# The borders of a feed-forward stage: VectorE's and ScalarE's orders by when TensorE needs each result, drains put off into the next pair, and two weight loads ahead of stores

## The reference, cut to what matters

```python
def swiglu_ffn(h, w_gate_up, w_down):
    gu = h @ w_gate_up                      # 1024 x 1024 by 1024 x 5632
    return (jax.nn.silu(gu[..., :D_FF]) * gu[..., D_FF:]) @ w_down   # D_FF = 2816
...
x = x + swiglu_ffn(rms_norm_2(x, norm_ffn[i]), ffn_w_gate_up[i], ffn_w_down[i])
return rms_norm_2(x, final_norm)
```

## Time and profile before

| what | value |
|---|---|
| median of three runs | 2220.53 us |
| the profiled execution | 2221.11 us, span 2219.3 us |
| TensorE matmul busy | 2047.9 us, 92% of the span |
| VectorE, ScalarE, GpSimd busy | 1422.1, 1007.3, 646.0 us |
| the stage `tail` (part with pairs) | 1540 to 2135 us of the span |
| TensorE's granted clock over the span | 0.958 of full |

### The profile page before, as it was taken

The page is one execution under the profiler, slowest core; times in us unless marked ns, Lnnn a source line. Parts: engine busy times, 40 slices in busy tenths (PEclk is TensorE's granted clock), DMA queues, the critical chain, the costliest instruction groups (busy, mean ns, idle before and its releaser), DMA issues. The chain is left out here.

```text
span 2219.3 us, 44505 instructions
## 1 busy us (share of the span) xinstructions
PE 2047.9 (92%) x15592; PEld 1533.1 (69%) x15592; DVE 1422.1 (64%) x1892; ACT 1007.3 (45%) x1513; POOL 646.0 (29%) x469
## 2 busy tenths in 40 slices
PE   5999989897598999988979989999899999999998
PEld 4788867686354555544558866678788888878787
DVE  6888627524578888877746448646755555474654
ACT  5212248302377788877722027723433333343334
POOL 1333311220000000000025632214444444454543
PEclk9999989998699999999979999999999999999999
DMA  7643114225999699999952310021233233264233
GB/s 275 239 164 126 39 52 167 107 77 219 401 420 422 254 391 423 422 422 422 380 190 95 95 34 1 1 95 57 81 100 105 98 113 99 85 229 145 100 122 125
DMA packets 100476, 410.06 MB, mean 185 GB/s; under 512 B 10444, under 2 KB 21548, under 8 KB 75436
## 3 DMA queue, kind: packets, MB, share of 16 engines
q1 hardware_dynamic: 81100, 366.53, 43.4%
q10 hardware_dynamic: 13968, 23.07, 2.8%
q0 software_dynamic: 5328, 19.40, 2.2%
HBM read 357.53 MB, written 51.43 MB: 184 GB/s over the span
## 5 line engine op out<-in xcount | busy, mean ns | idle before, releaser
L1712 PE MATMUL moe_hu<-x_res,acc_sq 128*32 128x256 f32 x5120 | 320.0, 392 | 25.0 <-DVE acc_sq L1631 12.4
L1609 DVE COPY x_res<-moew_raw 128x2048 f32 x243 | 269.7, 1136 | 105.8 <-PE moe_hu L1712 53.0
L1712 PEld LDWEIGHTS moe_hu<-x_res,acc_sq 128*32 128x32 f32 x5120 | 159.9, 112 | 144.4 <-issue 37.0
L1609 ACT ACTIVATE x_res<-moew_raw 128x2048 f32 (+1 forms) x121 | 197.9, 1636 | 34.2 <-DMA moew_raw<-in_w 24.0
L2584 PE MATMUL ff_bank<-xh,ff_u_hi 128*128 128x512 f32 x480 | 188.6, 393 | 9.9 <-DVE x_res L3065 6.6
L2546 POOL TENSOR_TENSOR ff_u_lo<-ff_sums,ff_u_hi 128x512 fp32r<-128x512 f32 x120 | 165.4, 1390 | 94.6 <-ACT ff_u_hi L2712 94.6
L2584 PE MATMUL ff_bank<-xh,ff_u_lo 128*128 128x512 f32 x480 | 187.5, 391 | 0.0
L2584 PE MATMUL ff_bank<-xl,ff_u_hi 128*128 128x512 f32 x480 | 187.5, 391 | 0.0
L2546 POOL TENSOR_TENSOR ff_u_lo<-ff_raw,ff_u_hi 128x512 fp32r<-128x512 f32 x90 | 122.9, 1366 | 215.2 <-ACT ff_u_hi L2712 215.2
L1620 ACT ACTIVATE moe_wdown<-moew_raw 128x2048 f32 x80 | 153.4, 1918 | 52.1 <-PE moe_y L1723 43.6
L1723 PE MATMUL moe_y<-moe_wdown,moe_at 128*32 128x256 f32 x2560 | 155.4, 384 | 2.2 <-ACT moe_at L1757 2.2
(11 more groups left out here) (489 smaller groups left out, 4615.7 us busy)
## 6 DMA issues: line engine op xcount, KB each, us to landing
moew_raw<-in_w SPq DMA_DIRECT2D x192, 1024.0 KB
ff_raw<-in_w_up SPq DMA_DIRECT2D x44, 512.0 KB, 3.6
blk_scratch<-x_res SPq DMA_DIRECT2D x56, 256.0 KB, 4.0
mid_w_raw<-in_w_qkv SPq DMA_DIRECT2D x24, 512.0 KB
in_w_raw<-in_w_in SPq DMA_DIRECT2D x23, 512.0 KB, 3.6
xbc<-in_w_ada SPq DMA_DIRECT2D x20, 512.0 KB, 8.5
y_scratch<-moe_ysb ACTq DMA_DIRECT2D x80, 128.0 KB, 6.8
ff_raw<-in_w_down SPq DMA_DIRECT2D x16, 512.0 KB, 3.6
```

Of the source, the lines that this page charges most:

```text
L1609: m = e.activation(to, src, ACT.Copy) if k == "act" else e.tensor_copy(to, src)
L1712: m = e.matmul(hu[u % 2][rows(j), 0:2 * FW].rearrange("p (a f) -> p a f", a=2), xt[:, t, rows(u)], w[:, :, FW * j:FW * (j + 1)], start=(t ...
```

## The change

The amount of computation stays the same on every engine. Orders and waits change.

- **SyncE, start of the stage.** `load_gate(2)` and `load_up(2)` are issued before the first store of pair 0; before, `load_up(2)` came behind it.
- **SyncE, first border.** `load_up(23)` comes before both stores of `LAST`.
- **ScalarE.** At the borders the blocks' high parts move to other places among the weights' high parts, and silu of `LAST`'s second half moves behind blocks 5 and 6.
- **VectorE, first border.** Blocks 0 to 3 are done before the first drain of pair 22. The rest of `LAST`'s gate moves into pair 22: the first half's `times_up` and the second half's sum behind drain p2, the second half's `times_up` behind drain p5.
- **VectorE, second border.** Blocks 0 to 3 are done in pair 25, and the drains p3, p5 and p6 of pair 25 move into pair 26.
- **Drains** now count on one semaphore, in the order of the list `drains`; `is_drained(e, c, p)` waits for the place of a drain in it. The four x tiles' wait is put on drains p2 and p6 as well.

```diff
+            drains = [(NPR, p) for p in range(7)]
+            for c in range(NPR + 1, NPR + NDN):
+                if c in borders:
+                    drains += [(c, p) for p in (0, 1, 2, 4)]
+                elif c - 1 in borders:
+                    drains += [(c, 0), (c, 1), (c, 2), (c - 1, 3), (c - 1, 5), (c, 3), (c, 4), (c, 5), (c - 1, 6), (c, 6)]
+                else:
+                    drains += [(c, p) for p in range(7)]
+            is_drained = lambda e, c, p: e.wait_ge(s_drained, drains.index((c, p)) + 1)
...
                     load_up(Q(1))
-                    after_even(Q(1))
+                    load_gate(Q(2))
+                    load_up(Q(2))
+                    store(Q(0), 0, 0, 0)
+                    store_mix(Q(0), 1)
...
                     load_block(0, 6)
+                    load_up(Q(NPR + 1))
                     store(LAST, 1, 0)
-                    load_up(Q(NPR + 1))
                     store(LAST, 1, 1)
...
+                    block_high(0, 0)
                     high(nq, 0)
                     high(nq, 1)
-                    block_high(0, 0)
+                    block_high(0, 1)
                     high(nq, 2)
                     high(nq, 3)
-                    block_high(0, 1)
+                    block_high(0, 2)
                     gate(q, 1, 0)
+                    block_high(0, 3)
                     high(nq, 4)
-                    block_high(0, 2)
                     high(nq, 5)
-                    gate(q, 1, 1)
-                    block_high(0, 3)
                     block_high(0, 4)
...
+                    def last_pair(n):
+                        if n == 0:
+                            sum_weights(pair_at(LAST, 1))
+                            block_low(0, 0)
+                            gate_sum(LAST, 1, 0)
+                            corner(LAST, 1)
+                            by_root(LAST, 1, 0, lambda: step.wait(e, LAST, 1), scaled)
+                            block_low(0, 1)
+                            block_low(0, 2)
+                            block_low(0, 3)
+                        elif n == 1:
+                            by_root(LAST, 1, 0, lambda: silu.wait(e, LAST, 1), step)
+                            times_up(LAST, 1, 0, 2)
+                        elif n == 2:
+                            gate_sum(LAST, 1, 1)
+                            by_root(LAST, 1, 1, lambda: step.wait(e, LAST, 3), scaled)
+                        else:
+                            by_root(LAST, 1, 1, lambda: silu.wait(e, LAST, 2), step)
+                            times_up(LAST, 1, 1, 4)
...
+                    def opening(c, left):
+                        n = borders[c - 1]
+                        drain(c, 0)
+                        block_low(n, 4)
+                        drain(c, 1)
+                        block_low(n, 5)
+                        drain(c, 2)
+                        left(0)
+                        drain(c, 3)
+                        block_low(n, 6)
+                        drain(c, 4)
+                        sum_weights(Q(c + 1))
+                        drain(c, 5)
+                        left(1)
+                        drain(c, 6)
+
+                    def inner(c):
+                        drain(c, 0)
+                        drain(c, 1)
+                        sum_weights(Q(c + 1), (0,))
+                        drain(c, 2)
+                        sum_weights(Q(c + 1), (1, 2, 3))
+                        for p in range(3, 7):
+                            drain(c, p)
+
+                    def ending(c):
+                        n = borders[c]
+                        drain(c, 0)
+                        drain(c, 1)
+                        sum_weights(Q(c + 1), (0,))
+                        drain(c, 2)
+                        sum_weights(Q(c + 1), (1, 2, 3))
+                        block_low(n, 0)
+                        drain(c, 4)
+                        for b in range(1, 4):
+                            block_low(n, b)
...
+                    def left_of_down(n):
+                        for p in ((3, 5), (6,))[n]:
+                            drain(NPR + FF_DOWN - 1, p)
```

More of the change, by code:

```diff
@@ L2391, in tail @@
             kept, scaled, silu, act_done = (PerPair(st, n, k) for n, k in (("kept", 3), ("scaled", 2), ("silu", 2), ("a", 2)))
-            c22, step, mixed, drained = (PerPair(st, n, k) for n, k in (("c22", 1), ("step", 4), ("mixed", 2), ("drained", 7)))
+            c22, step, mixed = (PerPair(st, n, k) for n, k in (("c22", 1), ("step", 4), ("mixed", 2)))
+            s_drained = st.sem("drained")
             halves = [(h, j) for h in range(2) for j in range(KT)]
@@ L2650, in _ @@
                             else:
-                                drained.wait(e, *{0: (before, 7), 1: (before, 6), 2: (d, 1), 3: (before, 4), 4: (d, 3), 5: (d, 2), 6: (d, 5)}[p])
+                                is_drained(e, *{0: (c - 2, 6), 1: (c - 2, 5), 2: (c, 0), 3: (c - 2, 3), 4: (c, 2), 5: (c, 1), 6: (c, 4)}[p])
                             if c - 1 in borders:
@@ L2836, in _ @@
                         high(q, 6)
+                        if c - 1 in borders:
+                            block_high(borders[c - 1], 5)
+                            block_high(borders[c - 1], 6)
                         if c == NPR:
-                            block_high(0, 5)
-                            block_high(0, 6)
-                        if c == NPR + FF_DOWN:
-                            block_high(1, 6)
+                            gate(LAST, 1, 1)
                         for p in range(6 if q != LASTD else 0):
                             high(pair_at(q, 1), p)
-                            if c == NPR + FF_DOWN - 1 and p < 5:
-                                block_high(1, p)
-                        if c == NPR + FF_DOWN - 1:
-                            block_high(1, 5)
+                            if c in borders and p in (0, 1, 3, 4, 5):
+                                block_high(borders[c], (0, 1, 2, 2, 3, 4)[p])
                     for k in range(FF_LAST):
@@ L2884, in _ @@
                     st.dve.start(e)
-                    for n in (summed, scaled, act_done, c22, step, mixed, drained):
+                    for n in (summed, scaled, act_done, c22, step, mixed):
                         n.start(e)
@@ L3052, in _, with drain @@
                         pair(Q(c), c % 2, mix=False)
-                    pair(LAST, 1, mix=False, between=lambda n: block_low(0, n))
-                    block_low(0, 2)
-                    def drain(q, p):
-                        d, (ja, jb) = down_pair(q), down_tiles(q)
+                    def last_pair(n):
[17 more added lines that the diff above has]
+                            times_up(LAST, 1, 1, 4)
+                    last_pair(0)
+                    def drain(c, p):
+                        q, (ja, jb) = Q(c), down_tiles(Q(c))
                         j, h = ((ja, 0), (jb, 1), (ja, 1), (ja, 0), (jb, 1), (ja, 1), (jb, 0))[p]
                         prod.wait(e, q, p + 1)
-                        if q[1] < NPR + FF_DOWN and j < K2 and p in (0, 1):
+                        if c < NPR + FF_DOWN and j < K2 and p in (0, 1, 2, 6):
                             e.wait_ge(s_kept[j], 32)
                         if p in (3, 4, 5):
-                            drained.wait(e, d, {3: 1, 4: 2, 5: 3}[p])
+                            is_drained(e, c, {3: 0, 4: 1, 5: 2}[p])
                         to = x[:, j, span(h)]
-                        drained.done(e.tensor_tensor(to, XYZ[q[1] % 2][(0, 1, 0, 2, 0, 1, 0)[p]], to, ALU.add))
+                        e.tensor_tensor(to, XYZ[c % 2][(0, 1, 0, 2, 0, 1, 0)[p]], to, ALU.add).then_inc(s_drained, 1)
                     def plane_low(k):
@@ new lines, in closing, with left_of_up @@
+                    def closing(c):
+                        for p in range(4):
+                            drain(c, p)
+                        plane_low(0)
+                        plane_low(1)
+                        drain(c, 4)
+                        plane_low(2)
+                        plane_low(3)
+                        drain(c, 5)
+                        plane_low(4)
+                        plane_low(5)
+                        drain(c, 6)
+                    def left_of_up(n):
+                        if n == 0:
+                            last_pair(1)
+                            last_pair(2)
+                        else:
+                            last_pair(3)
```

53 lines of the change are left out of this document (10 added, 43 removed).

## The result

The changed kernel takes 2224.62 us (median of 15 runs, 2218.18 to 2229.96), the kernel before beside it 2219.68 us (15 runs). The ratio is 1.0024, with a 95% interval of 1.0015 to 1.0033. The same kernel once more, beside other runs of before (2219.60 us), gave 2221.89 us and 1.0017 (1.0004 to 1.0030). I had expected it within 1.5 us of 2224.6, and it came 2.7 us lower. The change costs some 0.2%: both intervals lie above 1, the second barely.

The account below looks back on a forecast made before the run. TensorE, waiting for drains, was taken to set the end. Terms -2.15 + 5.1 + 2.0 - 0.9 = plus 4.05 us gave 2225.2 from the profiled execution, 2224.6 against the median; range 2216 to 2230.

Parts of the forecast that it names:

- no change: Whole kernel: a time from 2216.1 to 2225.0 us, within the 0.2% a measurement can tell; chance 0.42.
- rival (c): Pair 23: the jam comes but the clock stays up, or loads run at their lower bound; 2220.8 to 2222.6, chance 0.18.
- forecast case: Whole kernel: the prediction's own account holds, 2222.6 to 2229 us (later given as 2221 to 2229); chance 0.60.
- start of the stage: Pair 2's up weights, loaded ahead of the store, land sooner and VectorE's sums begin sooner: minus 2.15 us.
- first border up to pair 23: Pair 22: p2 starts sooner, p4 2.8 us late behind block 5; pair 23 starts at 1994.9, gaining 2.1 us.
- pair 23: wait and half clock: TensorE starts p4 of pair 23 7.0 us late, then runs at half clock for plus 2.0 us.
- second border: Pairs 25 to 27: earlier high parts shorten waits, p0 of pair 27 waits for a drain: minus 0.9 us.
- plus 5.1: Pair 24 starts at 2021.1 instead of 2016.0 us, from the late weights; bounds plus 1.8 to plus 7.7.
- the jam: SyncE's queue: late second store delays x loads to 2000.5 and pair 24's weights behind them; p4 of pair 23 7.0 late.
- GpSimd and VectorE take turns: First border: where both have work they alternate, a round of 3.5 us.
- Rival (a): Pair 24's weights land before VectorE's first sum, so the queue does not jam: 2215.4 us, chance 0.11.
- The clock behind it: TensorE's clock halves after the 7 us idle at pair 23: plus 2.0 us, from nothing to twice that.

Follow-up runs that it names:

- blocks_first: Changed kernel with blocks 5 and 6 of the first border loaded ahead of pair 23's gate weights in SyncE's list: 2218.78 us, again 2221.31 us.
- x_behind: Changed kernel with the wait for the last stores and the four x loads behind pair 24's weight loads in SyncE's list: 2215.24 us, ratio 0.9979.
- gate_early: Changed kernel with the last gate's remaining half ahead of pair 23's four weight sums on VectorE: 2218.64 us, ratio 0.9996.

## Why the prediction was right, by its own steps

The prediction was 2224.6 us, inside "no change" but next to "slower"; measured were 2224.62 and 2221.89. That it fits the first to the hundredth is luck: the two medians differ by 2.7 us, and against the kernel before beside them they are 4.9 and 2.3 us more, where 4.05 was predicted. By its own measure of 0.2% the first (1.0024) is just slower and the second (1.0017) no change. The second median lies in rival (c)'s range too, and in the forecast case's only as that is given at its second mention (2221 to 2229, at first 2222.6 to 2229); what (c) names, a clock that stays up or faster loads, its trace does not have. What is worth checking is the sum's terms.

| term | predicted | after | after, again |
|---|---|---|---|
| start of the stage | -2.15 | -1.0 | -2.2 |
| first border up to pair 23 | -2.1 | -1.3 | -1.0 |
| pair 23: wait and half clock | +7.0 and +2.0 | +6.6 and +1.5 | +7.0 and +3.0 |
| second border | -0.9 | -1.2 | -1.3 |
| sum | +4.05 | +4.7 | +5.5 |

(The prediction's "plus 5.1" is its second line and the 7.0 of the third, with 0.2 for the start-up of a matmul behind a wait.) The measured lines are differences of the losses to before's, with the first border's parted at the wait of pair 23.

**The start: mechanism right, the clock not thought of.** `load_up(2)` goes at the end of this row, near 1567.5, and the sums follow the gate op in front of them with no wait for a DMA:

```profile
1561.53 6.27 SPq L2436 DMA_DIRECT2D ff_raw<-in_w_up  x2
```

```profile
1575.45 0.69 DVE L2897 TENSOR_TENSOR x_res<-x_res 128x512 f32<-128x512 f32 x1
1576.07 0.68 DVE L2920 TENSOR_TENSOR ff_sums<-ff_raw 128x512 f32<-128x512 f32 x1
```

The 1.29 us wait is gone, and the 3.31 us one is 2.67. With the start-up of a matmul that is the predicted 2.2 us. VectorE did have one break on the way, 0.70 us for ScalarE behind the first gate sum, where the prediction said none; it stands in both kernels and changes nothing. Before ran at full clock behind its 3.31 us, and after at half behind its 2.67, which gives 1.2 back. In after's second trace the clock stayed up behind the same wait, and the start lost 7.9 us, 2.2 less than before. Of twelve executions with this edit two stayed up and ten fell.

**The first border up to pair 23: the place right, the gain too large.** "Before's clock" is here the time of after plus 7.42 us, 6.45 of the begin and 1.0 of the start. In it p2 of pair 22 starts at 1976.85, predicted 1977.5, before 1980.99. p4 waits 3.42 us where 2.8 were predicted, for the reason given: pair 23's gate load waited for GpSimd, and blocks 5 and 6 stood behind it. The predicted 0.5 us at p6 isn't there. The term that was left out is the half clock behind this wait too, which cost 1.5 us. Pair 23 starts at 1995.67 (1988.25 and 7.42), 1.3 us before its old 1996.96. blocks_first shows the cause of p4's wait, and that taking it away buys little while the jam stands behind it.

**GpSimd and VectorE take turns, as laid out.** VectorE's blocks 2 and 3 took 6.69 us as a merged pair, where one alone takes 2.29 (block 5, the second row), and GpSimd's ops lengthened beside them, in the two timelines of after:

```profile
1962.09 6.69 DVE L2897 TENSOR_TENSOR xl<-xl,xh 128x2048 fp32r<-128x2048 f32 x2
...
1975.64 2.29 DVE L2897 TENSOR_TENSOR xl<-xl,xh 128x2048 fp32r<-128x2048 f32 x1 [2.98 <-ACT xh L2825]
```

```profile
1963.29 3.34 POOL L2559 TENSOR_TENSOR ff_u_lo<-ff_raw,ff_u_hi 128x512 fp32r<-128x512 f32 x1
1966.59 6.62 POOL L2559 TENSOR_TENSOR ff_u_lo<-ff_sums,ff_u_hi 128x512 fp32r<-128x512 f32 x2
1973.17 1.29 POOL L2559 TENSOR_TENSOR ff_u_lo<-ff_raw,ff_u_hi 128x512 fp32r<-128x512 f32 x1
```

Three GpSimd ops took 3.3 us each beside VectorE's blocks, and 1.29 us once VectorE was idle (from 1972.66). The Trainium skill (SBUF — State Buffer, Who interferes with whom) calls the port pair that VectorE shares with GpSimd an exclusive lock. These rows fit it: the sum of both engines' work passes, not the longer of the two.

**The jam: right, link by link.** Predicted were a second store at 1998.2, x loads at 2000.5 and p4 of pair 23 7.0 us late. In before's clock the stores' row ends at 1999.5, the x loads go at 2001.3, and p4 is 6.6 us late. x_behind and gate_early take the wait away from either end of the chain. Rival (a) needed the second store before about 1991.5 in before's clock and is out. The figure of some 358 GB/s that the Trainium skill gives for HBM (DMA: Bandwidth & Descriptors, Where 436 GB/s comes from) would have made the sum 2223.4, which the totals can't tell from mine. The loads of the jam can: over the 7 us in which all six were under way they ran at 400 GB/s, so the figure did not bind here (columns as in the earlier trace rows).

```profile
1995.60:2002.60 7.00, 3.69 (x17) 2.72 (x15) 0.00 (x0) 0.02 (x1) 0.00 (x0) 0.96 1.02 400
```

**The clock behind it: right in kind, 1.5 and 3.0 us for 2.0.** From 2005.75 it took seven matmuls and 3.13 us to the first at full pace again, in place of 1.59: 1.5 us. In the second trace it was fourteen matmuls and 3.0 us, inside the bounds given.

**The second border: right, a little small.** 0.33, 0.85 and 0.97 us, the last at p0 of pair 27 behind the drain named, in place of 0.35, 1.29 and 1.76. Against this one execution of the old order it gains 1.2 us, against the two others 3 and more, since the half clock came there behind the old waits. The prediction had left the half clock out of this line.

## What to carry to other kernels

When an order is changed on one engine, follow each moved instruction to what it lets go on the others. Here one multiplication, moved from ahead of the first drain to behind the sixth, held SyncE's whole queue, and the weights in it, for 11.4 us; putting it ahead of four sums alone (gate_early) gave most of the loss back. A queue that works in order should have the loads that somebody is waiting for ahead of a wait for stores' landing, and a drain should not stand behind an operation that waits for a load. Compare single profiles from the start of the changed stage: here the untouched part of the program varied by more than the effect.

## What the runs showed of the hardware that I had not expected

**The clock isn't a function of the last wait alone.** Behind a wait of 3.31 us in the kernel before the granted clock was 1.00, behind 2.67 in after 0.50. In the two executions of one kernel, blocks_first, the matmuls behind a wait of 2.06 us went at full clock, and those behind one of 2.05 us at half:

```profile
1973.30:1976.50 3.20, 3.20 (x14) 2.65 (x15) 3.20 (x3) 1.93 (x1) 3.20 (x2) 1.00 0.06 24
```

```profile
1972.10:1975.30 3.20, 3.20 (x8) 2.55 (x9) 3.20 (x3) 1.91 (x1) 3.20 (x2) 0.52 0.10 40
```

In these thirteen executions no wait of 1.82 us or less at these places was followed by the half clock, and every one of 3.36 or more was. From 1.97 to 3.31 either came. The half clock then lasted six to fourteen matmuls and cost 1.5 to 3.0 us, so a wait of 2 us can cost nearly 4. It came at once behind some waits and a few matmuls later behind others, as behind the 1.97 us in gate_early. The same wait of 2.67 or 2.68 us at the start was followed by either clock in two executions of after. What decides in between I did not find.

**One order loses different amounts in different executions.** The first border of after lost 14.7 to 17.4 us in four, through the clock and through how long the same loads took to land. The earlier stages varied by 7.4 us in the start of pair 0 (1533.19 to 1540.58), with no change in them.
